# The second feed-forward block's down projection by seven products, its weight sums beside the mixer, and VectorE's order in such stages

## The reference, cut to what matters

```
def swiglu(x, w_gate, w_up, w_down):
    return (jax.nn.silu(x @ w_gate) * (x @ w_up)) @ w_down
...
    f = swiglu(rmsnorm(x, ffn2_pre_g[l]), ffn2_w_gate[l], ffn2_w_up[l], ffn2_w_down[l])
    x = x + 0.5 * rmsnorm(f, ffn2_post_g[l])
...
        mod = c_act @ ada_w[i] + ada_b[i]
        x = x + g2 * _swiglu(h, ffn_w_gate[i], ffn_w_up[i], ffn_w_down[i])
```

## Time and profile before

| | us |
|---|---|
| median of 3 runs (2676.91 to 2681.45) | 2679.58 |
| the profiled execution | 2679.96 |
| its span, first to last instruction | 2677.8 |
| TensorE busy | 2631.9 (98%) |
| VectorE busy | 1406.3 (53%) |
| ScalarE busy | 976.3 (36%) |
| GpSimd busy | 794.7 (30%) |

### The profile page before, as it was taken

One profiled execution on the slowest core, in us unless ns is written; L12 is line 12 of the kernel. 1 busy time (PEld: TensorE's weight loads), 2 busy tenths in 40 slices (PEclk: granted clock), 3 DMA queues, 4 the chain that ended last, 5 costly groups with the idle time before them and its releaser, 6 DMA issues.

```text
span 2677.8 us, 30627 instructions
## 1 busy us (share of the span) xinstructions
PE 2631.9 (98%) x12494; PEld 2144.2 (80%) x12494; DVE 1406.3 (53%) x2007; ACT 976.3 (36%) x1577; POOL 794.7 (30%) x654
## 2 busy tenths in 40 slices
PE   8999999999999999999999999999999999999999
PEld 7878888878777778887788766788888888888887
DVE  4344256656666544544524588563336844633366
ACT  4222143333544323422223444642225532422253
POOL 6564015665545568076700232010000000000000
PEclk9999999999999999999999998999999999999999
DMA  6544244444333355354433116899435623333355
GB/s 174 161 145 126 95 122 131 128 119 116 110 107 96 108 167 150 95 148 144 145 133 107 48 56 149 226 258 270 127 99 191 187 86 95 119 108 97 95 166 175
DMA packets 408620, 359.94 MB, mean 134 GB/s; under 512 B 16484, under 2 KB 336224, under 8 KB 408448
## 3 DMA queue, kind: packets, MB, share of 16 engines
q1 hardware_dynamic: 372720, 257.63, 32.5%
q0 software_dynamic: 34224, 98.78, 13.9%
q10 hardware_dynamic: 1536, 1.58, 0.2%
HBM read 354.23 MB, written 48.27 MB: 150 GB/s over the span
## 4 chain that ended last, share of the span: by engine, by line
PE 87%; DVE 8%; ACT 2%; DMA 1%; POOL 1%; issue 1%; SPq 0%; DVEq 0%; ACTq 0%; POOLq 0%
PE PS L504 18%; PE PS L505 18%; PE PS L507 16%; PE PS L582 4%; PE PS L584 4%; PE PS L583 4%; PE PS L509 2%; PE PS L635 2%; PE PS L637 2%; PE PS L638 2%; PE PS L1092 1%; PE PS L541 1%; PE PS L543 1%; PE PS L542 1%; PE PS L1064 1%; DVE WL L1895 1%
## 5 line engine op out<-in xcount | busy, mean ns | idle before, releaser
L504 PE MATMUL PS<-HH,WH 128*128 128x512 f32 x2248 | 897.9, 399 | 0.1
L505 PE MATMUL PS<-HL,WH 128*128 128x512 f32 x2248 | 875.4, 389 | 0.0
L507 PE MATMUL PS<-HH,WL 128*128 128x512 f32 x1967 | 766.7, 390 | 0.0
L1895 DVE TENSOR_TENSOR WL<-RAW,WH 128x1024 fp32r<-128x1024 f32 (+1 forms) x306 | 408.1, 1336 | 526.9 <-ACT WH L1183 526.4
L504 PEld LDWEIGHTS PS<-HH,WH 128*128 128x128 f32 x2248 | 422.9, 188 | 110.1 <-issue 25.6
L505 PEld LDWEIGHTS PS<-HL,WH 128*128 128x128 f32 x2248 | 423.1, 188 | 87.9 <-issue 4.6
L1183 ACT ACTIVATE WH<-RAW 128x1024 fp32r<-128x1024 f32 (+1 forms) x318 | 330.6, 1041 | 419.2 <-PE PS L509 346.0
L507 PEld LDWEIGHTS PS<-HH,WL 128*128 128x128 f32 x1967 | 369.7, 188 | 78.3
L2925 POOL TENSOR_SCALAR ADA<-ADA,CA 128x512 f32<-128x512 f32 x168 | 293.4, 1746 | 11.5 <-DMA ADA<-in_ada_w 4.0
L1895 DVE TENSOR_TENSOR WLr<-RAWD,WHr 128x1024 fp32r<-128x1024 f32 (+1 forms) x122 | 143.6, 1179 | 179.2 <-ACT WHr L1183 179.0
L2922 POOL TENSOR_TENSOR ASUM<-ASUM,ADA 128x512 f32<-128x512 f32 x168 | 231.0, 1375 | 14.0
(11 more groups left out here) (408 smaller groups left out, 3807.3 us busy)
## 6 DMA issues: line engine op xcount, KB each, us to landing
ADA<-in_ada_w POOLq DMA_DIRECT2D x192, 256.0 KB, 3.2
RAW<-in_ffn_w_gate SPq DMA_DIRECT2D x88, 512.0 KB, 4.0
RAW<-in_ffn_w_up SPq DMA_DIRECT2D x88, 512.0 KB, 4.0
RAW<-in_w_in SPq DMA_DIRECT2D x84, 512.0 KB, 3.9
RAWD<-in_ffn_w_down SPq DMA_DIRECT2D x74, 512.0 KB, 3.4
sum<-in_ffn_w_down POOLq DMA_DIRECT2D x12, 2816.0 KB, 22.5
RAWD<-sum SPq DMA_DIRECT2D x40, 512.0 KB, 4.1
RAW<-in_conv_w_in SPq DMA_DIRECT2D x24, 512.0 KB, 3.8
```

What stands on the lines that cost most here:

```text
L504: pe.matmul(PS[:, b, cols], wh[:, k, :], hi[:, k, cols], start=k == 0, stop=False)
L505: pe.matmul(PS[:, b, cols], wh[:, k, :], lo[:, k, cols], start=False, stop=False)
L507: pe.matmul(PS[:, b, cols], wl[:, k, :], hi[:, k, cols], start=False, stop=False)
L1895: return v.tensor_tensor(out, x, y, op).then_inc(*tick("dve", *event))
```

## The change

The down projection of f = 1 goes by seven products too: the plan has 42 chunks for it in place of 22, and four more sums stand in DRAM. GpSimd makes them between the modulation sums 8 to 19, one step of `make_sums`, now a generator, ahead of each even one. The fourth sums of f = 1 are made by VectorE, ahead of each near part. As its output is normed (r = 3 in NORMED), ScalarE takes squares of the whole output and VectorE scales and adds after them; the turns at r = 3 stand in the second row's pieces of the last product. In all product stages VectorE's tiles move behind chunk (7, 3), the gate at r = 5 behind near(3); at the end seventh(0) moves ahead of low_turned(r, 1), and the weights' low parts move back. ScalarE's second() waits for the tiles where r is in SHIFTED.

```diff
         cols(A["w_mlstm_branch"][0], n * P)
     second(A["w_out"][0], DK, "W")
-    swiglu(A["ffn2_w_gate"][0], A["ffn2_w_up"][0], A["ffn2_w_down"][0])
+    swiglu(A["ffn2_w_gate"][0], A["ffn2_w_up"][0], None)
+    by_products(1)
...
         for i in range(2, 6):
             piece(7, i, (0,))
-            if r < 7 and i in (3, 5):
+            if r in (5,) and i in (3, 5):
                 turn(r, i // 4)
         for i in range(2, 6):
             piece(7, i, (1,))
+            if r == 3 and i in (3, 5):
+                turn(r, i // 4)
...
         act(col(20 + tb), col(16 + tb), ACT.Sqrt, "xstd", r, tb, bias=eps, scale=1.0 / D)
 
+    def square_of(r, part, tb, b):
+        if (part, tb) != (0, 0):
+            w.wait_ge(*here("act"))
...
-            act(U8R[:, 4, pair(i), :], fourth_sum(m, i), ACT.Copy, "last", f, "hi", i)
+            act(U8R[:, 4, pair(i), :], fourth_sum(m, f, i), ACT.Copy, "last", f, "hi", i)
 
         def second():
+            if r in SHIFTED:
+                w.wait_ge(*at("tiles", r))
             w.wait_ge(*at("last", f, 1))
...
         a.activation(col(24), eps, ACT.Sqrt).then_inc(*tick("act"))
+        if r in NORMED:
+            upto(3, 2)
+            w.wait_ge(*at("last", f, 5))
+            for row in range(2):
+                w.wait_ge(*at("begun", r, row))
+                square_of(r, 0, row, row)
         upto(7, 1)
...
         highs(i0 + len(LOADED) + 0)
         if r == 7:
             return
+        if r in NORMED:
+            for row in range(2):
+                w.wait_ge(*at("upper right", r, row))
+                square_of(r, 0, 2 + row, 6 + row)
+            for row in range(2):
+                w.wait_ge(*at("whole", r, row))
+                square_of(r, 1, row, 4 + row)
+                deviation(r, row)
         square_x(r, 0)
         square_x(r, 1)
         highs(i0 + len(LOADED) + 1)
         high_turned(r, 0)
         highs(i0 + len(LOADED) + 2)
         high_turned(r, 1)
-        square_x(r, 2)
-        square_x(r, 3)
+        for row in range(2):
+            if r in NORMED:
+                w.wait_ge(*at("product", r, 7, row))
+                square_of(r, 1, 2 + row, 2 + row)
+                deviation(r, 2 + row)
+            square_x(r, 2 + row)
         high_turned(r, 2)
...
 
+        def fourth(i):
+            tt(fourth_sum(m, f, i), U8[:, A11, pair(i), :], U8[:, S3, pair(i), :], ALU.subtract, "fourth", f, i)
+
         def near(i):
+            if f == 1:
+                fourth(i)
             w.wait_ge(*at("fourth", f, i))
...
+
+        def normed_onto(tb, h0, b0, h1, b1):
+            w.wait_ge(*at("fs", r, 1, tb))
+            scaled(b1, h1)
+            w.wait_ge(*at("fstd", r, tb))
+            recip(col(12 + tb), col(12 + tb))
+            done()
+            stt(half_x(tb, h0), PS[:, b0, :], col(12 + tb), half_x(tb, h0), ALU.mult, ALU.add)
+            stt(half_x(tb, h1), PS[:, b1, :], col(12 + tb), half_x(tb, h1), ALU.mult, ALU.add, "x", r, tb)
...
-
-        done()
-        tt(fourth_sum(m, 5), U8[:, A11, pair(5), :], U8[:, S3, pair(5), :], ALU.subtract, "fourth", f, 5)
+            tt(U8R[:, S3, pair(i), :], fourth_sum(m, f, i), U8R[:, A11, pair(i), :].bitcast(F32), ALU.subtract, "last", f, i)
+
+        done()
+        if f > 1:
+            fourth(5)
         upto(2, 1)
         near(0)
         upto(6, 1)
-        if r == 5:
-            w.wait_ge(*at("gp", r))
-            w.wait_ge(*at("t0", r))
-            tt(GP[:, :, :], GP[:, :, :], m["T0"][:, :, :], ALU.add, "gate", r)
-        else:
-            tiles(r)
         upto(2, 2)
         near(1)
         upto(6, 2)
         near(2)
         upto(2, 3)
         near(3)
+        if r == 5:
+            w.wait_ge(*at("gp", r))
+            w.wait_ge(*at("t0", r))
+            tt(GP[:, :, :], GP[:, :, :], m["T0"][:, :, :], ALU.add, "gate", r)
         upto(6, 3)
         near(4)
...
         last(1)
         upto(7, 3)
-        if r == 5:
-            tiles(r)
+        tiles(r)
+        t.mark("dve", "tiles", r)
         upto(1, 3)
...
-        onto_sixth()
-        upto(4, 4)
-        done()
-        for row in range(2):
-            scaled(4 + row, 1)
-        upto(4, 5)
-        done()
-        for row in range(2):
-            onto(row, 1, 4 + row)
+        if r in NORMED:
+            w.wait_ge(*at("gp", r))
+        else:
+            onto_sixth()
+            upto(4, 4)
+            done()
+            for row in range(2):
+                scaled(4 + row, 1)
+            upto(4, 5)
+            done()
+            for row in range(2):
+                onto(row, 1, 4 + row)
         upto(3, 1)
         w.wait_ge(*at("product", r, 4, 1))
         for row in range(2):
             tt(PS[:, 2 + row, :], PS[:, row, :], E[:, row, :], ALU.add, "begun", r, row)
         upto(3, 2)
         done()
+        if r in NORMED:
+            upto(3, 3)
         for row in range(2):
+            if r in NORMED:
+                w.wait_ge(*at("fs", r, 0, row))
             scaled(row, 0)
         upto(3, 4)
         done()
-        for row in range(2):
-            onto(row, 0, row, "part", r, row, 0)
+        if r not in NORMED:
+            for row in range(2):
+                onto(row, 0, row, "part", r, row, 0)
         upto(7, 1)
         w.wait_ge(*at("product", r, 3, 1))
-        for row in range(2):
-            scaled(6 + row, 1)
-        done()
-        for row in range(2):
-            onto(row, 1, 6 + row, "x", r, row)
-        for row in range(2):
-            onto(2 + row, 1, 6 + row, "part", r, 2 + row, 1)
+        if r in NORMED:
+            for row in range(2):
+                tt(E[:, row, :], E[:, row, :], PS[:, 6 + row, :], ALU.add, "upper right", r, row)
+            w.wait_ge(*at("product", r, 6, 1))
+            for row in range(2):
+                done()
+                tt(PS[:, 4 + row, :], PS[:, 4 + row, :], E[:, row, :], ALU.add, "whole", r, row)
+            w.wait_ge(*at("fs", r, 0, 3))
+            ts(NB[:, 4:8], NB[:, 0:4], NORMED[r] / D, NORMED[r] * EPS, ALU.mult, ALU.add, "fs bias", r)
+            for row in range(2):
+                normed_onto(row, 0, row, 1, 4 + row)
+            for row in range(2):
+                scaled(6 + row, 1)
+        else:
+            for row in range(2):
+                scaled(6 + row, 1)
+            done()
+            for row in range(2):
+                onto(row, 1, 6 + row, "x", r, row)
+            for row in range(2):
+                onto(2 + row, 1, 6 + row, "part", r, 2 + row, 1)
         lows(i0 + len(LOADED) - 1)
 
         def seventh(row):
             w.wait_ge(*at("product", r, 7, row))
+            if r in NORMED:
+                normed_onto(2 + row, 1, 6 + row, 0, 2 + row)
+                return
             scaled(2 + row, 0)
             done()
...
         norm(r, 1)
         lows(i0 + len(LOADED) + 0)
         low_turned(r, 0)
+        seventh(0)
+        low_turned(r, 1)
         lows(i0 + len(LOADED) + 1)
-        low_turned(r, 1)
-        seventh(0)
-        lows(i0 + len(LOADED) + 2)
         norm(r, 2)
         seventh(1)
         norm(r, 3)
+        lows(i0 + len(LOADED) + 2)
         low_turned(r, 2)
         low_turned(r, 3)
...
+    ada_sums(5, 8)
+    first_sums = make_sums(g, tick, lambda *event: w.wait_ge(*at(*event)), A, 1)
+    for a in range(8, 20):
+        if a % 2 == 0:
+            next(first_sums)
+        ada_sums(a, a + 1)
     w.wait_ge(*at("y", 2, 3, 1))
...
     copy(0, quarter(A, f, 0, 0))
     copy(3, quarter(A, f, 0, 0))
+    yield
     wait("made", f, 0, "copied")
     add(0, quarter(A, f, 1, 0))
     wait("made", f, 3, "copied")
...
             w.wait_ge(*at("lo", j - NRAW))
-        for f, first in ((2, F3 + 2 * FK), (3, F4 + 2 * FK)):
+        for f, first in ((1, F2 + 2 * FK), (2, F3 + 2 * FK), (3, F4 + 2 * FK)):
             if 0 <= j - first < len(LOADED) and LOADED[j - first][0] in SUMS:
...
     for j in range(3, CHUNKS):
         load(j)
-        if j == F3 + 2 * FK + 8:
+        if j == F3 + 2 * FK + 11:
```

More of the change, by code:

```diff
@@ L195, in quarter @@
 def quarter(A, f, half, column):
-    w = A["ffn_w_down_2"][f - 2].rearrange("(j b p) n -> p j b n", b=2, p=P)
+    w = (A["ffn_w_down_2"][f - 2] if f > 1 else A["ffn2_w_down"][0]).rearrange("(j b p) n -> p j b n", b=2, p=P)
     return w[:, :, half, 512 * column:512 * column + 512]
 def sum_of(A, f, k):
-    return A["sums"][f - 2][k].rearrange("(j p) n -> p j n", p=P)
+    return A["sums"][f - 1][k].rearrange("(j p) n -> p j n", p=P)
 def factor(A, f, mul, i):
@@ L300 @@
 F1, MIX, BR1, BR2, WOUT, F2, DSA, DOUT, F3, CONV, COUT, F4, CHUNKS = (
-    0, 66, 135, 151, 167, 175, 241, 258, 266, 352, 376, 384, 470)
+    0, 66, 135, 151, 167, 175, 261, 278, 286, 372, 396, 404, 490)
 ON_POOL = range(DSA + 5, DOUT + 2)
@@ L348, in left_ready, with fourth_sum @@
     return {5: "near", 1: "near", 4: "later", 3: "later", 7: "last"}[mul], f, j // 2
-def fourth_sum(m, i):
+def fourth_sum(m, f, i):
+    if f == 1:
```

(27 more changed lines are left out.)

5 lines of the change are left out of this document (2 added, 3 removed).

## The result

The changed kernel took 2709.06 us (median of 4 runs, 2708.44 to 2711.28), the kernel before 2679.8 beside it: ratio 1.0112, 95% interval 1.01 to 1.0125. The forecast was 2702, with a range of 2676 to 2715: slower, as forecast, by 29 us where 22 were expected. The profiled execution took 2709.57, its span is 29.9 longer than before.

What follows compares the result with a forecast made beforehand. TensorE, busy 98% of the span, was taken as the bound. Terms -14.0 + 11.6 + 23.3 + 1.7 + 1.3 + 0.5 - 2.3 = +22.1 on 2679.96 gave 2702.1, forecast 2702; range 2676 to 2715.

Steps and rivals of the forecast that it cites:

- main mechanism: Beside the mixer, modulation loads wait behind the weight sums' DMAs in GpSimd's software queue, so TensorE waits for modulation sums.
- load behind the pair: GpSimd's modulation load behind two accumulating DMAs (39.7 us from 645.4) lands at 686.0; it was used at 650.46 before.
- Rival 1: Modulation's small loads slip past the accumulating DMAs at 645 to 690, landing within 12 us: 2676, chance 0.13.
- rival of the slower sums: Beside the weights the accumulating pair takes up to twice its 34.2 us, lengthening TensorE's wait: 2727, chance 0.05.
- sum 10: Modulation sum ready at 713.6, read by TensorE at 690.35: +23.3 us of wait, +1.7 for the clock.
- signs named: Near 20 us idle near 690, everything 25 to 28 later until the product stage of 107 to 108, head gap 6.
- Sum 16: Modulation sum whose load lands 9.1 us late behind one copy; ends at 987.7 before, read at 995.54: +1.3 us.
- Products: Second block's down projection loses 66 matmuls (15.0 us) and gains small waits, 107.5 for 121.5: -14.0 us.
- following VectorE's order chunk by chunk: Step sizing the second block's product-stage waits: two weight chunks 0.2 us late each, later two tile operations cost 0.6.
- Side effects: In the mixer, slowed weights' queue and the rotation's small DMAs: +0.5 us; as a rival 2712 to 2720, chance 0.10.
- The end of the stage: End of second block's product stage and next head: TensorE gaps 6.2 and 3.1, clock 2.5, less 0.2: +11.6 us.
- VectorE's order: Third and fourth blocks' product stages, gate and tiles moved back: -1.0, -0.9 and a head gap 0.35 shorter, -2.3 us.

Runs made afterwards that it cites:

- second trace: The changed kernel run once more, unedited, beside the follow-up runs: median 2710.73 us, ratio 1.0122 to the kernel before.
- stage end reordered: Changed kernel with second-row turns directly behind the products and ScalarE's and VectorE's order at the second block's product-stage end changed: 2703.01 us, ratio 1.0095.
- sums early: Changed kernel with make_sums' steps issued right behind modulation sums 7 to 13, before GpSimd waits for TensorE's read, the accumulating DMAs split: 2681.1 us, ratio 1.0012.

## Why the prediction was right, and where it was off

The sign and the main mechanism held. The load behind the pair was put at 686.0 and landed at 686.00, the wait at 23.3 and was 22.57, the clock at 1.7 and was 1.7. That the landing agrees so well is in part luck: the pair was issued at 647.05, 1.6 us later than assumed, and took 38.2 for 39.7. The windows of TensorE's clock show how that comes about (length, busy us by engine, granted clock, DMA share, GB/s):

```profile
686.00:692.00 6.00, 3.63 (x21) 2.65 (x20) 5.90 (x12) 3.68 (x5) 5.40 (x5) 1.00 1.20 298
692.00:698.00 6.00, 0.00 (x0) 0.00 (x0) 1.27 (x1) 0.00 (x0) 5.10 (x5) 0.51 0.58 166
...
710.00:716.00 6.00, 3.54 (x8) 1.66 (x9) 0.68 (x1) 0.59 (x1) 2.99 (x4) 0.50 0.16 46
716.00:722.00 6.00, 6.00 (x38) 5.25 (x37) 0.00 (x0) 2.65 (x5) 4.89 (x5) 1.00 0.29 88
```

TensorE is at half clock while it has nothing to do, which is free, and for 3.5 us after it resumes at 712.46, which costs half of them. The wait of 4.34 us costs no less: there the matmuls' pitch is 0.43 us until 1029.85 and 0.23 from 1030.16, 4.7 us after TensorE resumed, and 2.2 are lost.

Rival 1 is refuted at this place: the load did not slip past. The rival of the slower sums (2727) is refuted too, but the weights paid in its place. The issues and queues from 647 to 685:

```profile
q0 software_dynamic: 2948, 6.13, 86.8%
q1 hardware_dynamic: 2413, 1.22, 15.9%
...
RAW<-in_w_in SPq DMA_DIRECT2D x6, 512.0 KB, 17.5
```

Before the change q0 had 16.9% there and such a weight chunk landed in 3.8 us; now the median is 17.5. The two queues got about the same number of packets, 2948 and 2413, but one of the accumulating queue's holds four times the bytes and took 4.5 times as long (86.8/2948 against 15.9/2413). The Trainium skill (DMA: Bandwidth & Descriptors, Queues, rings and completion order) says that the turns go by packets, and the trace agrees as far as its own count goes: about equal in number, far from equal in time; whether a packet of the profile is one of the page's, no run shows. The kernel before had the same in the third block's sums: from 1781 to 1812 2559 and 2561 packets, 90.3% and 21.1% of the time, and weight chunks issued at 1773.90 and 1804.30 landed after 43.4 and 21.3 us. The price of the slow chunks could have been read there. The mixer could bear it, for it has four chunks ahead: TensorE has no idle stretch over 0.3 us from 650 until the wait at sum 10.

Of the signs named, the wait of near 20 us, the slow load and the head's first gap of 6 came; that all behind sum 10 would be 25 to 28 later did not: it is 23.8 later there and 33.2 at the product stage, which lasts 111.6 and not 107 to 108. The terms that were off, in order of size:

1. *Sum 16*, +1.3 against +6.6. The copy was as sized (12.4 for 13.1), and the load behind it 9.9 late. The steps behind it weren't followed: a further load came 1.66 late, and with the wait of 4.34 us the clock fell too, 2.2 of the kind that I had counted at sum 10 and not here.
2. *Products*, -14.0 against -9.9. The step that failed is "following VectorE's order chunk by chunk": I followed VectorE and not SyncE. A chunk came 11 us after its issue behind four tile loads; 2.17 of idle time, 0.4 later, and 1.7 of clock. Without that the stage is 107.7, the 107.5 of the sum. In the second trace of the same kernel the clock didn't fall there, and the term is -10.8.
3. *Side effects*, +0.5 against +4.4: 0.6 ahead of sum 8, 1.6 ahead of sum 14, 1.7 at a wait of 1.24 ahead of 1129, -0.4 at the next read of a sum, 0.8, -0.6 and 1.5 in sparse attention and the third block, -0.4 in the convolution. Most of it isn't the change's for certain. The 1.6 is no wait: the granted clock is 0.50 from 931.0 to 934.4 with TensorE busy throughout. The kernel before has two such falls between 720 and 1000, the changed one three, other kernels of the table none to three. The 1.5 (a wait of 1.16 ahead of 1869.11) is in this trace alone. Two traces of the same changed kernel differ by 4.7 in sparse attention (0.77 and 5.49 over the kernel before).
4. *The end of the stage*, +11.6 against +9.6. First gap 6.04 for 6.2, clock about 2.0 for 2.5; the second and third gaps 1.59 and 0.62 for 3.1 and 0.5. VectorE took the forecast's time, 10.0 us from the resumption to the end of its second weight chunk, for 10.2; but TensorE resumed there with that chunk, the low parts came beside its matmuls and cost 0.62 at the next place, and the matmuls before had run partly at half clock.
5. *VectorE's order*, -2.3 against -4.3. The head's gap fell by 0.4 as forecast (0.35), but the head is 1.7 shorter: with the gap went a fall of the clock, worth 1.3 and counted nowhere; before the change it followed the gap of 1.85, and none follows one of 1.45. The stage at r = 5 gave 1.65 for 1.0: the chunk behind the gate, put at 0.75 late, made no wait (2084.37).

With sum 10's -1.5 the errors of 5.3, 4.1, 3.9, -2.0 and -2.0 add up to +7.8, so the total is nearer than its terms are: three errors of 4 to 5 one way, three of 1.5 to 2 the other. In three of them (sum 16, products, VectorE's order) a fall of the clock, of 2.2, 1.7 and 1.3, was not priced with its gap; in the products the queue of SyncE, which only issues, was not walked.

## What to carry to other kernels

A large DMA added to a queue is paid for by the small one that stands behind it: put it where that engine waits for something else anyway, not where it next has work, and the same bytes cost 28 us less. Where a stage's end waits for one engine, write down all three queues from the last product on; to exchange two pieces of VectorE's work moved the wait (2.6 us less by the trace, nothing in the median), to reorder all three queues won 6.1 of 9.6. A change whose idea is right can lose by its placement: 66 matmuls less made the kernel 1.1% slower, and with three orders changed 0.3% faster than before.

## What the runs showed of the hardware

- On GpSimd's queue a small load lands behind the large DMA issued before it: a 256 KB load behind two accumulating DMAs of 2816 KB landed 0.75 us after the second, 36.7 us after its issue; behind one begun 14 us earlier, 8.7; behind a copy of 2816 KB, 13.5. The median is 3.2.
- With that queue full, the other queue's 512 KB loads landed in 17.5 us (median) and not in 3.8, at about equal packets.
- TensorE's granted clock was back at full speed 3.5 us after it resumed from 22.57 us of idleness, 4.7 us after it resumed from 4.34 (5.3 from 4.44 in the second trace) and 3.7 from 6.04 (2.7 in the second trace): a longer wait did not cost more clock. Shorter idle stretches don't settle it by their length: a fall followed those of 1.85 and 2.17, none followed 1.76 (1503.09, stage end reordered), 1.59 (1517.59, changed kernel) or 2.43 (627.74, sums early), and at the place of the 2.17 none followed 2.21 (1409.54, stage end reordered). And the kernel before shows falls of 3.4 us at 783 and 845 with no idle stretch over 0.6 us anywhere between 676 and 879.
